# Scattering a group's expert outputs back to tokens in fp32r high and low parts instead of fp32

## The chip, the cores and the metric

One core of a Trainium2 chip runs the whole kernel. The time is device microseconds of one execution; what counts is the median of the runs. A profiled execution gives the span (first to last instruction) and its own time.

## The reference

Two transformer blocks run one after the other over 256 tokens of width 1024. The first block ends in a mixture of experts: four groups of eight experts, a router picks one group for each token and two experts in it, and the weighted outputs are added to the tokens. Cut to what matters here:

```
g_sel = argmax(softmax(t @ w_rg + b_rg))            # one of 4 groups
top_p, top_i = top_k(softmax(e_logits of g_sel), 2) # two of its 8 experts
combine = one_hot(global_idx) * weights             # [tokens, 32]
for e in range(32):
    hid = silu(t @ w_gate[e]) * (t @ w_up[e])       # 1024 -> 256
    out = out + combine[:, e:e+1] * (hid @ w_down[e])   # 256 -> 1024
h = h + gt2 * out
```

After it come a final norm of the first block, then the second block: feed-forward passes (1024 to 2816 and back) over context and latents, attention, a convolution mixer and two more passes.

## The kernel before

**Weights.** All weights come as pages of 128 x 2048 fp32 (1 MB). A page for a three-product matmul is split: ScalarE (ACT) copies it to fp32r as the high part, GpSimd (POOL) subtracts that from the page and gives the low part, and TensorE (PE) forms high x high, high x low and low x high. The queue of SP issues the page loads in one written order, each behind waits on semaphores for the space it needs.

**The experts' stage.** Tokens are sorted by group into five groups of 128 rows (GSLOTS = 5, numbered j), and each group goes through the eight experts of its weights: 40 units (NUNIT), u = 8 j + e. A unit takes three expert pages (gate/up in two parts, and the down page), and in 32 of the 40 units (MOD_UNITS: all of the first 36 but every ninth) a modulation page (`mraw`) as well, which VectorE (DVE) multiplies by a vector and sums over k (`mod_sum`, into `MACC`), TensorE sums over partitions (`mod_product`) and VectorE adds to a table (`mod_take`). From unit 13 on the modulation pages are summed for two vectors, before for one.

TensorE's order in unit u (lines 1160 to 1186) is: first half of gate/up of u, transposing the hidden part of u-1, second half of gate/up of u, down of u-1 (fp32, 8 instructions of 512 columns, line 1146), `mod_product` of the page before, then one item of the groups' work: for group j-1 one quarter of the scatter (`scatter`, e = 1 to 4), or for group j+1 a gather (e = 5, 6) or `aux` (e = 7).

**The groups' work.** `onehot(j)` on VectorE writes the one-hot matrix EM (rows of a group by tokens), `gather` multiplies by it, `aux` transposes it in TensorE and `aux_copy` copies it to ET. After a group's last expert its outputs stand in PSUM banks 0 and 1, [128 rows, 1024]. `out_copy` on ScalarE copies them to OS in SBUF in two halves (line 1576), in unit 8(j+1) behind that unit's silu and two page splits. `scatter(j, r)` on TensorE multiplies quarter r of OS (two blocks of 128 columns as stationary operand) by ET (256 tokens), one fp32 matmul for each block, into bank 5; the profile shows an fp32 matmul as two instructions. `add_tokens(j, r)` on VectorE adds the result to the residual HT (line 2172), and each further quarter waits for the addition of the one before (semaphore s_scd). The fifth group has no unit behind it: its four quarters (`last_scatter`, line 1088) stand in the first feed-forward pass, between the first page's gate matmuls and the second's, and VectorE's `residual` takes them.

VectorE's order in unit u (lines 2184 to 2211) is: the hidden product HID (line 2191), `mod_sum` and `mod_take`, `add_tokens` (e = 1 to 4), `onehot` (e = 4), `gathered_lo` (e = 5, 6), `aux_copy` (e = 7). TensorE's `down(u)` for e = 0 waits until the banks were copied out (s_os), and `mod_product(m)` waits for `MACC` of page m (s_macc) and for the table entry before it (s_modev).

Of the kernel before, what the change touches and what calls it, by code (L numbers as in the profile page):

```python
# [20 lines left out]
P = 128  # L21
D = 1024
KD = D // P
S = 256
# [6 lines left out]
NG, NE8 = 4, 8  # L31
# [55 lines left out]
GSLOTS = S // P + NG - 1  # L87
# [5 lines left out]
def build(nc, pages, mpages, acts, vecs, mbias, small):  # L93
    f32, f32r, bf16, i32 = mybir.dt.float32, mybir.dt.float32r, mybir.dt.bfloat16, mybir.dt.int32
    ALU, ACT, AX = mybir.AluOpType, mybir.ActivationFunctionType, mybir.AxisListType

    ctx = ExitStack()
    with ctx:
        def sb(name, shape, dt=f32):
            return ctx.enter_context(nc.sbuf_tensor(name, shape, dt))  # L100
# [3 lines left out]
        def sem(name):  # L104
            if name not in sems:
                sems[name] = ctx.enter_context(nc.semaphore(name))
            return sems[name]
# [44 lines left out]
        LAMT = sb("LAMT", [P, 8])  # L152
        LAMV = MSK[:].rearrange("p (a b) -> p a b", a=4)
        ST = sb("ST", [P, 32])
        R = sb("R", [P, 11008])

        def reg(off, *dims, parts=P):
            n = int(np.prod(dims))
            v = R[0:parts, off:off + n]
            names = "abcd"[:len(dims)]  # L160
            if len(dims) == 1:
                return v
            return v.rearrange(f"p ({' '.join(names)}) -> p {' '.join(names)}",
                               **{names[i]: dims[i] for i in range(1, len(dims))})
# [19 lines left out]
        YT = reg(4096, TB, D)  # L184
        RW = reg(8192, 8, 80)
        EM = reg(8832, TB, P)
        ET = reg(9088, 2, S)
        OS = reg(9600, D)
        CWS = reg(10624, GSLOTS, NE8)
        IOTA, TRI, PIDX = CTf[:, 0:P], CTf[:, P:2 * P], CTf[:, 2 * P:2 * P + 1]  # L190
        GI = RW[:, 7, 64:64 + GSLOTS].bitcast(i32)
# [59 lines left out]
        def bias_of(h):  # L251
# [20 lines left out]
        s_mhi, s_mlo = sem("expert_page_hi"), sem("expert_page_lo")  # L272
        s_gu, s_gsil, s_ghid, s_gturn, s_ght, s_gdown = (sem("expert_gate_up"), sem("expert_silu"), sem("expert_hid"),
                                                         sem("expert_turned"), sem("expert_hid_copied"), sem("expert_down"))
        s_os, s_sct, s_scd = sem("group_out_copied"), sem("group_scattered"), sem("group_added")
        s_em, s_gat, s_xh, s_xl, s_aux, s_auxd = (sem("group_onehot"), sem("group_gathered"), sem("group_hi"), sem("group_lo"),
                                                  sem("group_aux"), sem("group_aux_copied"))
        s_silu = sem("silu_done")
# [160 lines left out]
        def opened(pe, name, i=0):  # L439

            if prev_free[name, i] is not None:
                pe.wait_ge(*prev_free[name, i])
            return bank(name, i)
# [226 lines left out]
        def _(pe):  # L670
# [388 lines left out]
            def aux(j):  # L1059
# [9 lines left out]
                              skip_group_check=True)  # L1069
                last.then_inc(s_aux, 1)  # L1070

            def scatter(j, r):
                if r == 0:
                    pe.wait_ge(s_os, 2 * (j + 1))
                    pe.wait_ge(s_auxd, 2 * (j + 2))
                else:
                    pe.wait_ge(s_scd, 4 * j + r)
                for b in range(2):
                    last = mm(PS[SPARE][:, b * S:(b + 1) * S], OS[:, (2 * r + b) * P:(2 * r + b + 1) * P], ET[:, j % 2, :],
                              start=True, stop=True, skip_group_check=True)  # L1080
                last.then_inc(s_sct, 1)

            def last_scatter():
                pe.wait_ge(s_os, 2 * GSLOTS)
                for r in range(4):
                    ps = opened(pe, "acc_moe", r)
                    for b in range(2):
                        last = mm(ps[:, b * S:(b + 1) * S], OS[:, (2 * r + b) * P:(2 * r + b + 1) * P],
                                  ET[:, (GSLOTS - 1) % 2, :], start=True, stop=True, skip_group_check=True)
                    last.then_inc(s_tile, 1)  # L1090

            def gate_up(u, ks):
                ps, x = PS[GATE_UP[u % 2]], (XGH[u // NE8 % 2], XGL[u // NE8 % 2])
# [44 lines left out]
            def down(u):  # L1138
                pe.wait_ge(s_ght, u + 1)
                pe.wait_ge(sem(f"expert_down_in_{u % 2}"), 16 * (u // 2 + 1))  # L1140
                if u % NE8 == 0 and u:
                    pe.wait_ge(s_os, 2 * (u // NE8))
                w = down_page(u)
                for j in range(2):
                    for n in range(2):
                        last = mm(PS[OUT[n]][:, :], HTT[:, j, :], w[:, j * D + n * 512:j * D + n * 512 + 512],  # L1146
                                  start=(u % NE8 == 0 and j == 0), stop=(u % NE8 == NE8 - 1 and j == 1), skip_group_check=True)
                last.then_inc(s_gdown, 1)
# [232 lines left out]
        def _(act):  # L1381
# [189 lines left out]
            def out_copy(j):  # L1571
                act.wait_ge(s_gdown, NE8 * (j + 1))
                if j:
                    act.wait_ge(s_sct, 4 * j)
                for n in range(2):
                    f(OS[:, n * 512:(n + 1) * 512], PS[n][:, :], ACT.Copy).then_inc(s_os, 1)

            for a in range(4):
                act.wait_ge(sem("tokens_turned"), a + 1)
# [147 lines left out]
        def _(dve):  # L1727
            v = nc.vector
# [18 lines left out]
            def mod_sum(m, vectors, i=0):  # L1747

                w = mraw[:, m % 2, :].rearrange("p (k n) -> p k n", k=KD)
                dve.wait_ge(mslot[m % 2], i * 16 + 16 * (m // 2 + 1 - MOD_AT["gates"] // 2))  # L1750
                if m:
                    dve.wait_ge(s_macc, i * 2 + m)
                for k in range(KD):
                    if k:

                        dve.wait_ge(s_mx, i * 2 * (KD - 1) + ((KD - 1) * m + k))
                    for slot_v, vi in enumerate(vectors):
                        part, c = PS[MISC][:, slot_v * FU:(slot_v + 1) * FU], CA[:, k, vi:vi + 1]
                        out = MACC[:, m % 2, slot_v, :] if k == KD - 1 else part
                        if k == 0:  # L1760
                            last = v.tensor_scalar(out, w[:, k, :], c, None, ALU.mult)
                        else:
                            last = v.scalar_tensor_tensor(out=out, in0=w[:, k, :], scalar=c, in1=part,  # L1763
                                                          op0=ALU.mult, op1=ALU.add)
                    last.then_inc(s_mx if k < KD - 1 else s_macc, 1)
# [69 lines left out]
            def modcol(c, vi=0):  # L1835
                return lambda k: MODT[:, c + k, vi:vi + 1]
# [318 lines left out]
            def gathered_lo(j, r):  # L2155
                dve.wait_ge(s_xh, 2 * j + r + 1)
                ps = PS[3] if j == 0 and r == 1 else PS[5]
                k = slice(4 * r, 4 * r + 4)
                v.tensor_tensor(XGL[j % 2][:, k, :], ps[:, :].rearrange("p (k n) -> p k n", k=4),
                                XGH[j % 2][:, k, :].bitcast(f32), ALU.subtract).then_inc(s_xl, 1)  # L2160
# [7 lines left out]
            def add_tokens(j, r):  # L2168
# [4 lines left out]
                                                  scalar=MODT[:, ADA + 40 + k, 0:1], in1=HT[:, k, :], op0=ALU.mult, op1=ALU.add)  # L2173
                last.then_inc(s_scd, 1)

            gathered_lo(0, 0)
            gathered_lo(0, 1)
            for n, (u, part) in enumerate(EARLY):
# [5 lines left out]
            for u in range(NUNIT):  # L2184
                j, e = u // NE8, u % NE8
                dve.wait_ge(s_gsil, u + 1)
                if u:
                    dve.wait_ge(s_gturn, u)
                if e == 0:
                    dve.wait_ge(s_auxd, 2 * (j + 1))  # L2190
                v.scalar_tensor_tensor(out=HID, in0=SIL[:, u % 2, :].rearrange("p (j n) -> p j n", j=2), scalar=CWS[:, j, e:e + 1],
                                       in1=PS[2 + u % 2][:, :].rearrange("p (j g n) -> p j g n", j=2, g=2)[:, :, 1, :],
                                       op0=ALU.mult, op1=ALU.mult).then_inc(s_ghid, 1)
                if u == 0:
                    mod_sum(20, (0,))
                if u in MOD_UNITS:
                    k = MOD_UNITS.index(u)
                    vectors = (0,) if k < MOE_ADA else (1, 2)
                    mod_sum(MOD_AT["moe"] + k, vectors)
                    mod_take(MOD_AT["moe"] + k - 1, 0, len(vectors))  # L2200
                if j and 1 <= e <= 4:
                    if e == 1 and j == 1:
                        dve.wait_ge(s_modev, (ADA + 48) // 2)
                    add_tokens(j - 1, e - 1)
                if j + 1 < GSLOTS:
                    if e == 4:
                        onehot(j + 1)
                    elif e in (5, 6):
                        gathered_lo(j + 1, e - 5)
                    elif e == 7:  # L2210
                        aux_copy(j + 1)
                if u == NUNIT - 3:
                    norm_head(2)
                if u == NUNIT - 2:
                    norm_tiles(2, range(0, 5), low=False)
                if u == NUNIT - 1:
                    norm_tiles(2, range(5, KD), low=False)
                    for q in range(KD):
                        norm_low(2, q)
            residual("acc_moe", (HT, modcol(ADA + 40)))  # L2220


# [304 lines left out]
```

## Time and profile before

| | |
|---|---|
| runs | 2069.66, 2064.40, 2061.06 us; median 2064.4 |
| profiled execution | 2073.07 us, span 2071.3 us, granted clock 0.979 |
| TensorE busy | 1976.6 us, 95% of the span |
| GpSimd busy | 1379.1 us, 67% |
| VectorE busy | 981.7 us, 47% |
| ScalarE busy | 827.7 us, 40% |
| DMA | 473.80 MB, mean 229 GB/s |
| experts' stage | from about 250 to 715 us of the span |

Busy times of one engine overlap with those of others. A matmul's duration is longer than the distance to the next one, since they are pipelined; what a matmul costs is the distance of starts. PEld is the load of the stationary operand. A clock of 1.00 is TensorE's full 2.4 GHz.

### The profile page before, as it was taken

To read this page: it belongs to the slowest core of one execution; us is meant where nothing else is said; L and a number is where in the kernel's file an instruction comes from. 1 tells how busy PE (TensorE), PEld (TensorE's weight loads), DVE (VectorE), ACT (ScalarE), POOL (GpSimd) and SP (SyncE) were. 2 spreads that over 40 slices of the span, in tenths; PEclk is the share of its full clock that TensorE was granted. 3 is DMA by queue.
4 is the path that set the end of the run, shared out by engine and by line. 5 is a ranking of instruction groups with operands and counts; after the bars stand their busy time and mean duration, and the time that the engine had idled before them with its cause. 6 is when DMAs were issued, how large, how long until landed. Compare 5 with 4: busy or idle time off the path is not lost.

```text
span 2071.3 us, 34705 instructions
## 1 busy us (share of the span) xinstructions
PE 1976.6 (95%) x13854; PEld 1780.4 (86%) x13854; DVE 981.7 (47%) x2149; ACT 827.7 (40%) x873; POOL 1379.1 (67%) x321
## 2 busy tenths in 40 slices
PE   6999799999999999999999999899999999999998
PEld 4879766677676799999999768689999999999998
DVE  6766453567676354345335243453335334642112
ACT  4443344444434554334434333343344334434332
POOL 5727078778778677787775412277776776766884
PEclk9999899999999999999999999999999999999999
DMA  8636299989998656665664302156665565554542
GB/s 354 227 121 265 100 359 365 372 343 377 360 382 334 257 204 227 241 243 217 250 236 167 123 27 96 45 220 244 242 236 200 237 236 229 221 187 160 184 182 82
DMA packets 67407, 473.80 MB, mean 229 GB/s; under 512 B 8064, under 2 KB 9184, under 8 KB 10208
## 3 DMA queue, kind: packets, MB, share of 16 engines
q1 hardware_dynamic: 65344, 466.82, 59.0%
q10 hardware_dynamic: 1952, 5.44, 0.7%
q8 instruction: 78, 1.28, 0.2%
q14 instruction: 33, 0.27, 0.0%
HBM read 471.18 MB, written 1.05 MB: 228 GB/s over the span
## 4 chain that ended last, share of the span: by engine, by line
PE 49%; issue 23%; POOL 18%; DMA 5%; DVE 2%; ACT 1%; SPq 0%; POOLq 0%; ACTq 0%; DVEq 0%
POOL W L606 15%; PE bank L675 11%; PE bank L677 11%; PE bank L676 11%; PE bank L1146 4%; DMA raw<-in_pages 4%; PE bank L681 2%; PE bank L683 2%; PE bank L682 2%; POOL YC L657 2%; POOL W L657 1%; PE bank L709 1%; PE bank L700 1%; PE bank L1055 1%; DMA mraw<-in_mpages 1%
## 5 line engine op out<-in xcount | busy, mean ns | idle before, releaser
L606 POOL TENSOR_TENSOR W<-raw,W 128x2048 fp32r<-128x2048 f32 x220 | 1013.9, 4613 | 528.9 <-ACT W L1436 528.8
L675 PE MATMUL bank<-YH,W 128*128 128x256 f32 x1936 | 551.2, 285 | 1.4 <-POOL W L606 1.1
L677 PE MATMUL bank<-YH,W 128*128 128x256 f32 x1936 | 547.7, 283 | 0.0
L676 PE MATMUL bank<-YL,W 128*128 128x256 f32 x1936 | 547.6, 283 | 0.0
L1436 ACT ACTIVATE W<-raw 128x2048 fp32r<-128x2048 f32 x220 | 420.2, 1910 | 300.6 <-PE bank L677 274.6
L675 PEld LDWEIGHTS bank<-YH,W 128*128 128x128 f32 x1936 | 371.1, 192 | 4.2 <-POOL W L606 1.5
L676 PEld LDWEIGHTS bank<-YL,W 128*128 128x128 f32 x1936 | 371.3, 192 | 0.4 <-issue 0.2
L677 PEld LDWEIGHTS bank<-YH,W 128*128 128x128 f32 x1936 | 371.2, 192 | 0.0
L1763 DVE SCALAR_TENSOR_TENSOR bank<-mraw,CA,bank 128x256 f32<-128x256 f32 x702 | 331.5, 489 | 20.3
L1860 DVE TENSOR_TENSOR bank<-bank,SIL 128x256 f32<-128x256 f32 x110 | 47.6, 432 | 574.6 <-ACT SIL L1455 574.6
L675 PE MATMUL bank<-HH,W 128*128 128x256 f32 x880 | 249.4, 283 | 0.4 <-DVE HL L1862 0.4
L677 PE MATMUL bank<-HH,W 128*128 128x256 f32 x880 | 245.7, 279 | 0.0
L676 PE MATMUL bank<-HL,W 128*128 128x256 f32 x880 | 245.3, 279 | 0.0
L657 POOL TENSOR_TENSOR W<-raw,W 128x2048 fp32r<-128x2048 f32 x38 | 173.2, 4580 | 84.6 <-ACT W L1558 84.6
L1558 ACT ACTIVATE W<-raw 128x2048 fp32r<-128x2048 f32 x79 | 151.2, 1915 | 147.1 <-DMA raw<-in_pages 147.1
L657 POOL TENSOR_TENSOR YC<-raw,W 128x2048 fp32r<-128x2048 f32 x36 | 163.9, 4576 | 43.9 <-ACT W L1558 43.9
L1455 ACT ACTIVATE SIL<-bank 128x256 f32<-128x256 f32 x110 | 42.2, 384 | 361.6 <-PE bank L677 359.3
L681 PE MATMUL bank<-W,YH 128*128 128x512 f32 (+1 forms) x392 | 154.4, 394 | 14.7 <-POOL YC L657 7.3
L675 PEld LDWEIGHTS bank<-HH,W 128*128 128x128 f32 x880 | 165.7, 188 | 0.6 <-issue 0.4
L676 PEld LDWEIGHTS bank<-HL,W 128*128 128x128 f32 x880 | 165.6, 188 | 0.0
L677 PEld LDWEIGHTS bank<-HH,W 128*128 128x128 f32 x880 | 165.4, 188 | 0.0
L675 PE MATMUL bank<-YC,W 128*128 128x256 f32 (+1 forms) x536 | 153.6, 287 | 1.0 <-DVE R L1950 1.0
(348 smaller groups left out, 3130.9 us busy)
## 6 DMA issues: line engine op xcount, KB each, us to landing
raw<-in_pages SPq DMA_DIRECT2D x299, 1024.0 KB, 4.9
mraw<-in_mpages SPq DMA_DIRECT2D x98, 1024.0 KB, 7.0
R<-in_pages SPq DMA_DIRECT2D x24, 1024.0 KB, 6.3
XR<-in_pages SPq DMA_DIRECT2D x17, 1024.0 KB, 6.3
R<-in_mpages SPq DMA_DIRECT2D x4, 1024.0 KB, 16.4
HT<-in_acts ACTq DMA_DIRECT2D x1, 1024.0 KB, 14.2
CT<-in_mpages SPq DMA_DIRECT2D x1, 1024.0 KB, 19.4
raw<-in_mpages SPq DMA_DIRECT2D x1, 1024.0 KB, 25.2
```

The costliest lines, as they stand in the source:

```text
L606: nc.gpsimd.tensor_tensor(WL[:, p % SLOTS, :], raw[:, p % SLOTS, :], WH[:, p % SLOTS, :].bitcast(f32), ALU.subtract).then_inc(s_lo, 1)
L657: p_.tensor_tensor(PAIRL[u % 2][:, part].rearrange("p k n -> p (k n)"), expert_raw(u, part), PAIRH[u % 2][:, part, :].bitcast(f32), ALU.su ...
L675: mm(out, w[0], x[0], start=start, stop=False, skip_group_check=True)
L676: mm(out, w[0], x[1], start=False, stop=False, skip_group_check=True)
L677: return mm(out, w[1], x[0], start=False, stop=stop, skip_group_check=True)
L681: mm(out, x[0], w[0], start=start, stop=False, skip_group_check=True)
L1146: last = mm(PS[OUT[n]][:, :], HTT[:, j, :], w[:, j * D + n * 512:j * D + n * 512 + 512], start=(u % NE8 == 0 and j == 0), stop=(u % NE8 == ...
L1436: f(WH[:, p % SLOTS, :], raw[:, p % SLOTS, :], ACT.Copy).then_inc(s_hi, 1)
L1455: f(SIL[:, j, :], PS[GU[j]][:, 0:S], ACT.Silu).then_inc(s_silu, 1)
L1558: f(PAIRH[u % 2][:, part, :], expert_raw(u, part), ACT.Copy).then_inc(s_mhi, 1)
L1763: last = v.scalar_tensor_tensor(out=out, in0=w[:, k, :], scalar=c, in1=part, op0=ALU.mult, op1=ALU.add)
L1860: step(v.tensor_tensor(hid, hid, sil, ALU.mult))
```

## The change

The scatter's two operands become fp32r. ScalarE's copy of the group's outputs writes fp32r (OSH), VectorE gets a new step `out_low` that subtracts it from the PSUM banks and writes the low part (OSL, fp32r), and each scatter block is two fp32r matmuls, high and low, against one ET, which is fp32r now too (its copy on VectorE writes that type). RR is a second name for the memory of R; OSL lies in a part of it that the stage does not use. What waited on s_os for the copies (scatter's first quarter, `down` of a group's first unit, the last scatter) waits on s_osl for the subtractions. `out_low(j-1)` stands in VectorE's order behind HID of unit 8j and ahead of that unit's `mod_sum`; for the last group it stands ahead of `residual`.

```diff
-        ET = reg(9088, 2, S)
-        OS = reg(9600, D)
+        ET = RR[:, 9088:9600].rearrange("p (a t) -> p a t", a=2)
+        OSH, OSL = RR[:, 9600:9600 + D], RR[:, 2048:2048 + D]
...
+            def to_tokens(ps, j, r):
+                for b in range(2):
+                    k = 2 * r + b
+                    mm(ps[:, b * S:(b + 1) * S], OSH[:, k * P:(k + 1) * P], ET[:, j % 2, :], start=True, stop=False,
+                       skip_group_check=True)
+                    last = mm(ps[:, b * S:(b + 1) * S], OSL[:, k * P:(k + 1) * P], ET[:, j % 2, :], start=False, stop=True,
+                              skip_group_check=True)
+                return last
+
             def scatter(j, r):
                 if r == 0:
-                    pe.wait_ge(s_os, 2 * (j + 1))
+                    pe.wait_ge(s_osl, 2 * (j + 1))
                     pe.wait_ge(s_auxd, 2 * (j + 2))
                 else:
                     pe.wait_ge(s_scd, 4 * j + r)
-                for b in range(2):
-                    last = mm(PS[SPARE][:, b * S:(b + 1) * S], OS[:, (2 * r + b) * P:(2 * r + b + 1) * P], ET[:, j % 2, :],
-                              start=True, stop=True, skip_group_check=True)
-                last.then_inc(s_sct, 1)
+                to_tokens(PS[SPARE], j, r).then_inc(s_sct, 1)

             def last_scatter():
-                pe.wait_ge(s_os, 2 * GSLOTS)
                 for r in range(4):
...
+                    if r % 2 == 0:
+                        pe.wait_ge(s_osl, 2 * (GSLOTS - 1) + r // 2 + 1)
+                    to_tokens(opened(pe, "acc_moe", r), GSLOTS - 1, r).then_inc(s_tile, 1)
...
                 if u % NE8 == 0 and u:
-                    pe.wait_ge(s_os, 2 * (u // NE8))
+                    pe.wait_ge(s_osl, 2 * (u // NE8))
...
-                    f(OS[:, n * 512:(n + 1) * 512], PS[n][:, :], ACT.Copy).then_inc(s_os, 1)
+                    f(OSH[:, n * 512:(n + 1) * 512], PS[n][:, :], ACT.Copy).then_inc(s_os, 1)
...
+            def out_low(j):
+                if j:
+                    dve.wait_ge(s_sct, 4 * j)
+                for n in range(2):
+                    half = slice(n * 512, (n + 1) * 512)
+                    dve.wait_ge(s_os, 2 * j + n + 1)
+                    v.tensor_tensor(OSL[:, half], PS[n][:, :], OSH[:, half].bitcast(f32), ALU.subtract).then_inc(s_osl, 1)
...
                 if u == 0:
                     mod_sum(20, (0,))
+                if j and e == 0:
+                    out_low(j - 1)
                 if u in MOD_UNITS:
...
+            out_low(GSLOTS - 1)
             residual("acc_moe", (HT, modcol(ADA + 40)))
```

## Rows read from the trace of the kernel before

**Rows 1.** Page, parts 1 and 4: busy times; the chain by engine.

```profile
PE 1976.6 (95%) x13854; PEld 1780.4 (86%) x13854; DVE 981.7 (47%) x2149; ACT 827.7 (40%) x873; POOL 1379.1 (67%) x321
...
PE 49%; issue 23%; POOL 18%; DMA 5%; DVE 2%; ACT 1%; SPq 0%; POOLq 0%; ACTq 0%; DVEq 0%
```

**Rows 2.** Windows: engines' busy us (instructions), PE clock, DMA share, GB/s; experts' stage.

```profile
350.00:430.00 80.00, 75.98 (x314) 55.16 (x313) 45.91 (x89) 33.45 (x31) 67.35 (x15) 0.96 0.90 352
430.00:520.00 90.00, 89.32 (x387) 63.71 (x386) 63.91 (x145) 38.87 (x37) 73.06 (x17) 1.00 0.92 369
...
600.00:710.00 110.00, 104.01 (x429) 72.96 (x430) 57.82 (x133) 53.03 (x58) 79.49 (x20) 0.98 0.81 317
...
730.00:900.00 170.00, 169.63 (x1403) 168.66 (x1401) 74.56 (x163) 76.31 (x74) 127.70 (x29) 1.00 0.62 229
```

**Rows 3.** Timeline of PE: start, us, what, count; the last scatter and after.

```profile
714.64 3.61 PE L1088 MATMUL bank<-R 128*128 128x256 f32 x16
717.90 0.47 PE L675 MATMUL bank<-YC,W 128*128 128x256 f32 x1
718.21 0.28 PE L676 MATMUL bank<-YC,W 128*128 128x256 f32 x1
...
720.48 0.28 PE L677 MATMUL bank<-YC,W 128*128 128x256 f32 x1
```

**Rows 4.** Timeline of PE: units 17 and 25, then later starts behind waits [idle].

```profile
450.76 3.60 PE L1146 MATMUL bank<-R,WRT 128*128 128x512 f32 x8
454.19 0.95 PE L700 MATMUL bank<-ONES,MACC 128*128 128x1 f32 x8
...
466.85 0.50 PE L681 MATMUL bank<-W,YH 128*128 128x512 f32 x1 [0.68 <-POOL YC L657]
...
542.50 0.95 PE L700 MATMUL bank<-ONES,MACC 128*128 128x1 f32 x8
...
567.04 0.50 PE L681 MATMUL bank<-W,YH 128*128 128x512 f32 x1 [1.39 <-POOL W L657]
...
569.19 0.39 PE L681 MATMUL bank<-W,YH 128*128 128x512 f32 x1
...
624.86 0.80 PE L681 MATMUL bank<-W,YH 128*128 128x512 f32 x1 [1.91 <-POOL YC L657]
...
628.53 0.40 PE L681 MATMUL bank<-W,YH 128*128 128x512 f32 x1
...
635.65 0.50 PE L700 MATMUL bank<-ONES,MACC 128*128 128x1 f32 x4
...
666.74 3.70 PE L1146 MATMUL bank<-R,WRT 128*128 128x512 f32 x8 [1.51 <-ACT WRT L1569]
```

**Rows 5.** Timeline of ACT: the output copies of four groups.

```profile
357.07 1.06 ACT L1576 ACTIVATE R<-bank 128x512 f32<-128x512 f32 x2
...
448.08 1.07 ACT L1576 ACTIVATE R<-bank 128x512 f32<-128x512 f32 x2
...
536.26 1.06 ACT L1576 ACTIVATE R<-bank 128x512 f32<-128x512 f32 x2
...
628.07 1.06 ACT L1576 ACTIVATE R<-bank 128x512 f32<-128x512 f32 x2
```

**Rows 6.** Timeline of DVE: sum in unit 16, one-hots of units 12 and 28.

```profile
399.94 4.16 DVE L2123 TENSOR_SCALAR R<-R 128x2 f32<-128x2 f32 x1
...
441.71 0.86 DVE L1761 TENSOR_SCALAR bank<-mraw,CA 128x256 f32<-128x256 f32 x2
...
448.11 0.87 DVE L1763 SCALAR_TENSOR_TENSOR MACC<-mraw,CA,bank 128x256 f32<-128x256 f32 x2
...
583.32 4.70 DVE L2125 TENSOR_SCALAR R<-CT,R 128x128 f32<-128x128 f32 x2
```

**Rows 7.** Groups of DVE by form: the like of the new subtraction.

```profile
L2159 DVE TENSOR_TENSOR YL<-bank,YH 128x512 fp32r<-128x512 f32 x10 | 6.9, 685 | 8.3 <-ACT YH L1563 8.3
```

**Rows 8.** Timeline of POOL: the two page subtractions beside unit 28's one-hot.

```profile
578.62 9.12 POOL L657 TENSOR_TENSOR W<-raw,W 128x2048 fp32r<-128x2048 f32 x2 [2.56 <-ACT W L1558]
```

More of the change, by code:

```diff
@@ L154, in build @@
         ST = sb("ST", [P, 32])
+        with nc.sbuf_tensor("RR", [P, 11008], f32r) as RR:
+            pass
         R = sb("R", [P, 11008])
@@ L274, in build @@
                                                          sem("expert_turned"), sem("expert_hid_copied"), sem("expert_down"))
-        s_os, s_sct, s_scd = sem("group_out_copied"), sem("group_scattered"), sem("group_added")
+        s_os, s_osl, s_sct, s_scd = (sem("group_out_high"), sem("group_out_low"), sem("group_scattered"),
+                                     sem("group_added"))
         s_em, s_gat, s_xh, s_xl, s_aux, s_auxd = (sem("group_onehot"), sem("group_gathered"), sem("group_hi"), sem("group_lo"),
@@ L1077, in scatter @@
                     pe.wait_ge(s_scd, 4 * j + r)
-                for b in range(2):
-                    last = mm(PS[SPARE][:, b * S:(b + 1) * S], OS[:, (2 * r + b) * P:(2 * r + b + 1) * P], ET[:, j % 2, :],
-                              start=True, stop=True, skip_group_check=True)
-                last.then_inc(s_sct, 1)
+                to_tokens(PS[SPARE], j, r).then_inc(s_sct, 1)
             def last_scatter():
-                pe.wait_ge(s_os, 2 * GSLOTS)
                 for r in range(4):
[L1086 to L1090, printed above, removed]
+                    if r % 2 == 0:
+                        pe.wait_ge(s_osl, 2 * (GSLOTS - 1) + r // 2 + 1)
+                    to_tokens(opened(pe, "acc_moe", r), GSLOTS - 1, r).then_inc(s_tile, 1)
             def gate_up(u, ks):
```

## The prediction

> **What bounds the kernel now.** I read the page first, for the bound as a whole: TensorE is busy 95% of the span, POOL 67%, and the chain that ended last is half TensorE [rows 1]. Then the windows, because the change lies in the experts' stage only, from about 260 to 720 us. There TensorE is busy 76.0 of 80 us, 89.3 of 90 and 104.0 of 110, while the DMA engines are busy 81 to 92% and move 317 to 369 GB/s [rows 2]. So two limits stand close together in this stage: TensorE sets the end of most units, and now and then a page lands late and TensorE waits for POOL's low part. The reader is to see those waits in TensorE's timeline: 0.68 us at 466.85, 1.39 at 567.04, 1.91 at 624.86, 1.51 at 666.74 [rows 4]. Behind the stage TensorE is the bound outright, 169.6 of 170 us [rows 2].
>
> **TensorE's part of the change.** The last scatter has 16 instructions (8 fp32 matmuls of two each). From its first start at 714.64 to that of the fp32r matmul behind it at 717.90 are 3.26 us, 0.204 each; with the odd step to 718.21 in it, less one fp32r distance, 3.45 us, 0.216 each. I take 0.21 us [rows 3]. An fp32r matmul of the same shape goes at the distance of starts of the pass behind it: 19 steps from 718.21 to 720.48, 0.1195 us [rows 3]. The new form has as many instructions as the old, since each block is a high and a low matmul: 4 in place of 4 in a quarter, 16 in place of 16 in the last scatter. Each loses 0.21 - 0.12 = 0.09 us. A quarter saves 0.36 us, 16 quarters save 5.8 us, the last scatter saves 1.44 us: 7.2 us in all. The bounds are 0 (if fp32r with these operands went at fp32's 0.21 us) and 7.2; I take 7.2, since the neighbouring row is of the same shape and type. The Trainium skill, page TensorE: Matmul & The Clock Gate, section "Wait — 56ns, not 53.3ns?", gives a warm distance of the columns over 2.4 GHz and some 2.5 ns, 109 ns for 256 columns. The rows say 0.1195, and the measurement decides; by the page the whole saving would be an estimated 0.8 us larger.
>
> ScalarE's copy only changes its output type, and so does VectorE's copy to ET: both cost nothing, hidden as before.
>
> **VectorE's part.** `out_low` adds two subtractions of 128x512 from PSUM to fp32r for each group, ten in all. The like of it takes 685 ns, with a mean over ten instances [rows 7]: 1.37 us a group, 6.9 us in all. VectorE is 47% busy [rows 1] and 63.9 of 90 us in its fullest window [rows 2], so the work itself is hidden. What counts is where it waits. It waits for ScalarE's copies, which run far behind the unit's silu, because two page splits stand ahead of them: they start at 357.07, 448.08, 536.26 and 628.07 and take 1.06 us [rows 5]. Behind the waiting `out_low` stands the unit's `mod_sum`, and for it waits `mod_product` on TensorE one unit later.
>
> Unit 16: `mod_sum` ran from 441.71 to 448.98, 7.27 us [rows 6]. Now the first copy (half of 1.07 us) is there at 448.6, the subtractions end at 448.6 + 1.37 = 450.0, the sum runs to 457.3. TensorE's `down` of that group at 450.76 finds its banks free 0.8 us before it needs them. Its `mod_product` stood at 454.19 [rows 4] and now waits until 457.3: 3.1 us. Unit 24: copies from 536.26, subtractions to 538.2, sum to 545.5; `mod_product` stood at 542.50 [rows 4, 5]: 3.0 us. Unit 32: 628.07, 630.0, 637.3, against 635.65: 1.6 us. Unit 8: subtractions to 359.0, a sum for one vector behind them, and unit 9 has no page and so no product: no wait. Sum of the new waits: 7.7 us.
>
> After a wait the clock may fall. Behind the 1.91 us of idle, nine starts from 624.86 to 628.53 took 3.67 us, at half clock for most of them; behind the 1.39 us of idle, nine starts from 567.04 to 569.19 took 2.15 us [rows 4]. So a fall costs 1.5 us. I charge it for the two waits of 3 us and not for the one of 1.6, which lies between an idle of 1.51 without a fall and one of 1.91 with it.
>
> What else is late behind VectorE's delay is covered: HID of unit 17 comes behind the sum, near 458, and the transposing that needs it stands in TensorE's order behind `mod_product` (now 457.3), a scatter and half a gate/up. `add_tokens` of the first quarter stands behind one more sum of 7.3 us, near 466; the second quarter stood just ahead of 466.85 [rows 4] and the stall moves it too. The SP queue holds page loads behind `s_macc` of two pages before; these sums are done long before their turn. For the last group `out_low` ends at 710.5 on an idle VectorE, and the scatter cannot start before the first page's gate matmuls end at 714.64 [rows 3]: nothing.
>
> **Sum, by group.** Quarters of group 0 (units 9 to 12): -1.44, but the page behind unit 12 and the one-hot behind it (4.16 us of waiting in its first instruction [rows 6]) set the next start, so I keep -0.7. Group 1: +3.1 wait, +1.5 clock, -0.68 because the wait at 466.85 is swallowed, -1.44 scatters: +2.5. Group 2: +3.0 + 1.5 - 1.39 (the wait at 567.04) - 1.44: +1.7. Group 3: TensorE arrives later by then, so half of the 1.91 + 1.5 us around 624.86 goes: -1.7; its own wait of 1.6, less three quarters' gain, vanishes in the 1.51 us at 666.74; the fourth quarter gives -0.36. Last scatter: -1.44, kept in full, since TensorE bounds what follows [rows 2]. Together -0.7 + 2.5 + 1.7 - 1.7 - 0.36 - 1.44 = 0.0 us. The profiled execution would stay at 2073 us, 8.7 us above the runs' median (0.4%); on the median that is 2064.4 + 0.0, so about 2064 us: no change.
>
> **Rivals.**
> A. The waits do not form (VectorE's sums keep their lead, or the pages of these units land so late that TensorE is not there to wait), and the gain is kept: 2064.4 - 7.2 = 2057.2 us. For it: VectorE idles much. Against: `mod_sum` of unit 16 ended only 5.2 us before its use [rows 4, 6], and it moves by 8.3.
> B. The waits are paid in full: three waits of 7.7 us, three falls of the clock of 4.5 us, nothing covered, against 7.2 gained: +5.0, 2069.4 us. For it: the kernel issues the next pages behind TensorE's `down`, so a late TensorE makes the pages late too. It decides from the point where the waits at 567.04 and 624.86 come back as long as before.
> C. The one-hot on VectorE falls behind one more subtraction of POOL. The row of unit 28: two small instructions take 4.70 us and end at 588.0 just behind POOL's pair, which ended at 587.74, 4.56 us for each [rows 6, 8]; the gather on TensorE stands right behind them. VectorE's order moves against POOL's by some us, and where it gets to the one-hot just after POOL has started another page, TensorE waits up to 4.56 + 1.5 us. Twice, on top of the forecast: +12.1, 2076.5 us: the case on the other side, slower. Against: by units 20 and 28 VectorE has caught up, and POOL's times follow the same pages. The Trainium skill, page SBUF — State Buffer, section "Who interferes with whom", has the rule for this: an operation such as tensor_scalar in a two-port mode and a GpSimd instruction exclude one another for a whole instruction. The trace agrees, by the 4.70 and 4.16 us.
> D. The change doesn't do what it says: fp32r products with these operands take fp32's time, and 7.2 us go missing: 2071.6 us. Against: 0.1195 us in every fp32r pass of this shape.
>
> **Chances.** Forecast (2061 to 2068) 0.60, A 0.13, B 0.14, C 0.08, D 0.05. A measurement of this kernel can tell about 0.5%, 10.3 us, from no change: below 2054.1 or above 2074.7. A lies inside that unless chance runs add to it; the three runs of before spread from -3.3 to +5.3 us about their median. Faster 0.08, same 0.80, slower 0.12 (C and the upper end of B and D). The range of 8 in 10 is 2056 to 2073: it takes in A and B with their spread, and leaves out C.
>
> **What would show it.** Right: L1079's and L1088's successors as fp32r at 0.12 us each, the last scatter at 1.9 us in place of 3.4; ten new VectorE subtractions of 0.69 us; an idle of TensorE ahead of `mod_product` (L700 in before's numbering) in units 17 and 25 near 3 us, released by VectorE's MACC, with half clock behind it; the waits in units 19 and 28 gone. Wrong: no such idle and an experts' stage shorter by 6 us (A); the old waits unchanged beside the new (B); a gather waiting for the one-hot (C).

## The result: slower by 0.67%

The changed kernel took 2080.54 us (median of 6 runs, 2079.34 to 2085.12), the kernel before 2066.3 us (6 runs, 2061.06 to 2071.89). The ratio is 1.0067, 95% interval 1.005 to 1.0084: some 14 us slower, where 2064 us and no change were forecast, with a range up to 2073. The profiled execution took 2080.16 us, span 2078.3 us, granted clock 0.977.

### The profile page after: what moved, and what is told of

Its sections match the earlier page's. It is cut to its first block, busy times and chain, and to the rows that moved or that the text cites. A ratio compares the mean times of both kernels' runs of the same rounds, so it can differ in the third digit from the quotient of the medians.

```text
span 2078.3 us, 34720 instructions
## 1 busy us (share of the span) xinstructions
PE 1975.6 (95%) x13854; PEld 1779.9 (86%) x13854; DVE 993.1 (48%) x2159; ACT 826.6 (40%) x873; POOL 1379.3 (66%) x321
## 4 chain that ended last, share of the span: by engine, by line
PE 46%; issue 24%; POOL 18%; DMA 6%; DVE 4%; ACT 1%; SPq 0%; POOLq 0%; ACTq 0%; DVEq 0%
POOL W L609 15%; PE bank L678 11%; PE bank L680 11%; PE bank L679 11%; DMA raw<-in_pages 4%; PE bank L1152 3%; PE bank L684 2%; PE bank L685 2%; PE bank L686 2%; DVE bank L1769 2%; POOL YC L660 1%; DMA mraw<-in_mpages 1%; PE bank L712 1%; PE bank L703 1%; POOL W L660 1%
## 5 line engine op out<-in xcount | busy, mean ns | idle before, releaser
L684 PE MATMUL bank<-W,YH 128*128 128x512 f32 (+1 forms) x392 | 152.9, 390 | 11.8 <-DVE W L2194 4.3
```

The lines of the kernel that those rows point to most:

```text
L684: mm(out, x[0], w[0], start=start, stop=False, skip_group_check=True)
```

## The profile after

The page's first and fourth part, as in [rows 1]. TensorE has the same number of instructions and is busy for 1 us less; VectorE has ten instructions more and 11 us more. The chain has less TensorE in it (46% for 49%) and more VectorE (4% for 2%).

```profile
PE 1975.6 (95%) x13854; PEld 1779.9 (86%) x13854; DVE 993.1 (48%) x2159; ACT 826.6 (40%) x873; POOL 1379.3 (66%) x321
...
PE 46%; issue 24%; POOL 18%; DMA 6%; DVE 4%; ACT 1%; SPq 0%; POOLq 0%; ACTq 0%; DVEq 0%
```

TensorE's work in the last scatter, from its timeline, against [rows 3]: 16 instructions from 725.86 on, 15 steps in 1.79 us, 0.119 us each. This term of the sum is as forecast.

```profile
725.86 0.28 PE L1078 MATMUL bank<-RR 128*128 128x256 f32 x1
...
727.65 0.28 PE L1080 MATMUL bank<-RR 128*128 128x256 f32 x1
```

The new subtractions, from the groups of VectorE (busy, mean ns | idle before, by what). They cost what [rows 7] said, 686 ns. The 39.3 us are VectorE's waits for ScalarE's copies.

```profile
L2188 DVE TENSOR_TENSOR RR<-bank,RR 128x512 fp32r<-128x512 f32 x10 | 6.4, 686 | 39.3 <-ACT RR L1582 39.3
```

Where TensorE waited between 250 and 720 us: the view of waits, after (us in total, times, longest). L703 is the modulation product, L1152 the down matmuls, L684 gate/up, L1058 the gather.

```profile
PE bank L703 <- DVE MODT L1778: 10.1, 3, 3.6
PE bank L684 <- DVE W L2194: 4.3, 1, 4.3
PE bank L684 <- POOL YC L660: 3.7, 4, 1.9
PE bank L1152 <- DVE RR L2188: 3.6, 3, 1.4
PE bank L684 <- POOL W L660: 3.6, 3, 1.7
PE bank L1058 <- DVE R L2131: 2.8, 2, 1.6
PE bank L1152 <- ACT WRT L1575: 1.1, 1, 1.1
```

And before:

```profile
PE bank L681 <- POOL YC L657: 7.3, 4, 2.3
PE bank L681 <- DVE W L2180: 4.3, 1, 4.3
PE bank L1146 <- ACT WRT L1569: 3.3, 3, 1.5
PE bank L681 <- POOL W L657: 3.1, 2, 1.7
PE bank L1055 <- DVE R L2125: 1.7, 1, 1.7
```

Two lines are new, 10.1 us at the product and 3.6 us at the down matmuls. Those for POOL and ScalarE went from 13.7 to 8.4 us, so it looks as if 5.3 us of the new waits replace old ones. That is a comparison of one profile with one; two more profiles of the changed kernel, from the experiments below, have 9.7 + 0.8 us (`e1_after`) and 10.4 + 2.2 us (`e4_after`) of new waits beside 7.3 and 9.8 us of old ones. The wait at the product is the steady part.

How one such wait comes about: units 16 and 17 after, first ScalarE, then VectorE, then TensorE (start, us, what; in brackets the idle before).

```profile
439.26 0.38 ACT L1601 ACTIVATE SIL<-bank 128x256 f32<-128x256 f32 x1 [1.62 <-PE bank L686]
445.03 1.92 ACT L1564 ACTIVATE W<-raw 128x2048 fp32r<-128x2048 f32 x1 [5.38 <-DMA raw<-in_pages]
447.62 1.92 ACT L1564 ACTIVATE W<-raw 128x2048 fp32r<-128x2048 f32 x1 [0.67 <-DMA raw<-in_pages]
449.44 1.06 ACT L1582 ACTIVATE RR<-bank 128x512 fp32r<-128x512 f32 x2
```

```profile
450.12 1.29 DVE L2188 TENSOR_TENSOR RR<-bank,RR 128x512 fp32r<-128x512 f32 x2 [9.96 <-ACT RR L1582]
451.33 0.86 DVE L1767 TENSOR_SCALAR bank<-mraw,CA 128x256 f32<-128x256 f32 x2
...
457.73 0.87 DVE L1769 SCALAR_TENSOR_TENSOR MACC<-mraw,CA,bank 128x256 f32<-128x256 f32 x2
458.51 0.15 DVE L1778 TENSOR_TENSOR MODT<-bank,MB 128x4 f32<-128x4 f32 x1
```

```profile
451.56 3.67 PE L1152 MATMUL bank<-R,WRT 128*128 128x512 f32 x8 [1.45 <-DVE RR L2188]
458.82 1.17 PE L703 MATMUL bank<-ONES,MACC 128*128 128x1 f32 x8 [3.59 <-DVE MODT L1778]
459.85 0.56 PE L1078 MATMUL bank<-RR 128*128 128x256 f32 x1
460.20 0.41 PE L1080 MATMUL bank<-RR 128*128 128x256 f32 x1
...
460.85 0.63 PE L684 MATMUL bank<-W,YH 128*128 128x512 f32 x1
...
462.98 0.39 PE L686 MATMUL bank<-W,YH 128*128 128x512 f32 x1
```

ScalarE's copies stand behind two page splits, and those behind the landing of their pages: 10.2 us after unit 16's silu. VectorE idles 9.96 us for them with the modulation sum queued behind. TensorE first waits for the subtractions at the down matmuls (1.45 us), then for the sum at the product (3.59 us). Unit 33 shows the same pair, 1.29 and 3.59 us. The second number is the same because, once the down matmuls are held by the subtractions, both engines start from there: the sum and its table entry take 7.3 us, the down matmuls 3.7 us, and the difference is TensorE's wait. Behind it the clock is at half: the scatter's steps are 0.21 us, no faster than fp32 was. So are the first gate/up matmuls, 0.42 us a step until 462.98 and 0.23 behind.

From one unit's silu to the next is the length of a unit. I add the stage from unit 0's silu to unit 39's (before 263.68 to 698.96, after 265.65 to 710.18).

| kernel (one profile each) | 17 to 18 | 25 to 26 | 33 to 34 | stage |
|---|---|---|---|---|
| before | 10.95 | 10.95 | 10.95 | 435.3 |
| before, product later (`e3_before_late`) | 10.90 | 10.89 | 10.89 | 430.6 |
| changed | 17.13 | 15.25 | 18.69 | 444.5 |
| changed, again (`e1_after`) | 16.68 | 17.01 | 16.98 | 445.7 |
| changed, again (`e4_after`) | 15.53 | 18.68 | 17.38 | 445.1 |

## The experiments

Theory W: it is VectorE's order. The subtraction waits for the copies, the sum waits behind it, TensorE waits for both. Rival P: the time goes elsewhere; a faster scatter moves TensorE against the pages, and the pages set the end. Every comparison is with the kernel before on the same chip.

**The changed kernel again**, twice, unedited (`e1_after`, `e4_after`).

> The changed kernel as it is, beside the next three. Theory W (order of VectorE): the low subtraction waits some 10 us for ScalarE's copies with the modulation sum behind it, TensorE then waits at the down matmuls and at the modulation product of units 17, 25 and 33, some 4 to 8 us a time. Both theories: about 2080 us, ratio 1.007 to the kernel before.

2084.02 us, ratio 1.0058 (1.0035 to 1.0081); stage 445.7 us.

**Subtractions behind the sum** (`e1_behind`).

```diff
-                if j and e == 0:
-                    out_low(j - 1)
                 if u in MOD_UNITS:
...
                     mod_take(MOD_AT["moe"] + k - 1, 0, len(vectors))
+                if j and e == 0:
+                    out_low(j - 1)
```

> out_low moved behind mod_sum and mod_take in VectorE's order, nothing else. Theory W: the waits at the modulation product vanish; the copies end some 10 us after the silu and the sum some 8 to 9 us after it, so the subtractions are done hardly later than now and a wait of 1 to 3 us at the down matmuls may stay; 2062 us, between 2057 and 2067, ratio 0.996 to 1.001. Rival P (the time goes elsewhere: the faster scatter shifts TensorE against the pages' landing and the pages set the end): no change from 2080 us.

2065.66 us, ratio 0.9993 (0.9981 to 1.0006). The whole loss is gone with an order of two steps, and nothing of the scatter was touched: P falls. No line for the product is left in the waits; the down matmuls wait 0.2 us for the subtractions. Units 17, 25 and 33 take 10.54, 10.58 and 10.94 us, the stage 430.4.

**Copies ahead of the page splits** (`e1_copyfirst`).

```diff
+                j, e = u // NE8, u % NE8
+                if j and e == 0:
+                    out_copy(j - 1)
                 if u + 2 < NUNIT:
                     expert_split(u + 2, 0)
                     expert_split(u + 2, 1)
-                j, e = u // NE8, u % NE8
-                if j and e == 0:
-                    out_copy(j - 1)
```

> ScalarE's out_copy moved ahead of the unit's two page splits, VectorE's order as in the changed kernel. Theory W: the copies no longer wait for pages; they start when the down matmuls of the group before end, 3.5 us after the silu, the sum ends about 13 us after the silu and the product is wanted at about 14: all waits gone, 2060 us, between 2056 and 2066. If the two splits start later by it (the pages land 2.3 us or more after the silu), up to 2 us a group come back. Rival P: 2080 us.

2064.19 us, ratio 0.9982 (0.9966 to 0.9997). VectorE's order is the changed kernel's, so it was not that the subtraction stood ahead of the sum, but that it waited there for copies held by pages. In unit 16 VectorE's idle is now 3.24 us, and the product does not wait:

```profile
442.78 1.29 DVE L2188 TENSOR_TENSOR RR<-bank,RR 128x512 fp32r<-128x512 f32 x2 [3.24 <-ACT RR L1582]
...
450.38 0.87 DVE L1769 SCALAR_TENSOR_TENSOR MACC<-mraw,CA,bank 128x256 f32<-128x256 f32 x2
```

```profile
452.71 0.95 PE L703 MATMUL bank<-ONES,MACC 128*128 128x1 f32 x8
```

**VectorE's part alone, in the kernel before** (`e1_lowonly`): fp32 scatter; the low values are computed and waited for, and nothing reads them.

```diff
+                    v.tensor_tensor(OSL[:, half], PS[n][:, :], OS[:, half], ALU.subtract).then_inc(s_osl, 1)
...
-                    pe.wait_ge(s_os, 2 * (j + 1))
+                    pe.wait_ge(s_osl, 2 * (j + 1))
...
+                if j and e == 0:
+                    out_low(j - 1)
```

> The kernel before with VectorE's low subtraction added and waited for as in the changed kernel, but the scatter stays fp32 and reads the high part's place (OS in fp32) alone; the low values are written and read by nothing. Theory W: it has all of the loss and none of the gain of 7 us: 2085 to 2092 us, ratio 1.010 to 1.014. Rival P: no loss without the faster scatter, 2066 us.

2080.07 us, ratio 1.0053 (1.0032 to 1.0073); waits at the product 8.9 us in three, stage 446.9. The loss is there without the fp32r scatter. I had expected 2085 to 2092 us, the changed kernel's time and the missing gain of 7 us on top, and that did not come: the ratio is level with `e1_after`'s 1.0058, each with an interval of some 4 us to either side. While the waits stand, the scatter's gain does not show in this comparison; no run says why.

**The gain side alone** (`e2_highonly`).

```diff
-                    last = mm(ps[:, b * S:(b + 1) * S], OSL[:, k * P:(k + 1) * P], ET[:, j % 2, :], start=False, stop=True,
+                    last = mm(ps[:, b * S:(b + 1) * S], OSH[:, k * P:(k + 1) * P], ET[:, j % 2, :], start=False, stop=True,
...
-                    pe.wait_ge(s_osl, 2 * (j + 1))
+                    pe.wait_ge(s_os, 2 * (j + 1))
...
-                if j and e == 0:
-                    out_low(j - 1)
```

> The changed kernel without VectorE's low subtraction: it leaves the low part out and takes the high part in its place, so the scatter has the same number of fp32r matmuls, and its waits are those of the kernel before (on ScalarE's copies). This is the gain side alone. Theory W with the forecast's size: 80 instructions at 0.12 in place of 0.21 us, -7.2 us at most, 2060 us, ratio 0.996 to 0.998. Rival P (in this stage the pages set the end, so a shorter scatter is given back): -1.5 us, what the last scatter gives, ratio 0.999 to 1.000.

2063.2 us, ratio 0.9968 (0.9953 to 0.9983), which is 6.6 us, 3.5 to 9.7. The forecast's 7.2 us lie inside, and the 1.5 us of rival P outside. The low part is left out here, so this kernel is only good for its time.

**Product half a gate/up later** (`e2_late`), and its controls without the change (`e3_before_late`) and with the fp32 scatter and unread low values (`e3_lowonly_late`).

```diff
+            def product(u):
+                k = MOD_UNITS.index(u)
+                mod_product(MOD_AT["moe"] + k - 1, 0, 1 if k < MOE_ADA else 2)
...
                     gate_up(u, range(0, KD // 2))
+                    if u > 10 and u % NE8 == 2 and u - 1 in MOD_UNITS:
+                        product(u - 1)
                     turn_hid(u - 1)
...
-                if u in MOD_UNITS:
-                    k = MOD_UNITS.index(u)
-                    mod_product(MOD_AT["moe"] + k - 1, 0, 1 if k < MOE_ADA else 2)
                 j, e = u // NE8, u % NE8
+                if u in MOD_UNITS and not (u > 9 and e == 1):
+                    product(u)
```

> The changed kernel with TensorE's modulation product of units 17, 25 and 33 put half a gate/up later (behind scatter and the first half of the next unit's gate/up, 3.2 us). VectorE's order is left as it is. If the wait at the product is the larger part of the loss, most of it goes: 2070 us (2066 to 2074). If the wait at the down matmuls and the fall of the clock behind it carry the loss, it stays at 2078 to 2084.

> The kernel before with TensorE's product of units 17, 25 and 33 half a gate/up later: the control for e2_late. The sum is done 5 us before the product is wanted there, so nothing should change: ratio 0.999 to 1.001. If it gives 0.998 as e2_late did, that gain is the order's and not the scatter's.

> The kernel before with VectorE's low subtraction (fp32 scatter, the low values read by nothing) and the product half a gate/up later. With e1_lowonly it says how much of the subtraction's loss is the product's wait, with e2_late what the fp32r scatter gives once that wait is gone. Theory W: the loss of 12 us shrinks to 0 to 3 us, 2068 to 2071 us, ratio 1.000 to 1.0015, and the fp32r scatter is worth the 4 to 6 us between this and e2_late. If the scatter's gain is given back to the pages in any case, it comes out level with e2_late, 0.998.

`e2_late`: 2065.19 us, ratio 0.9981 (0.9968 to 0.9993), better than the 2070 expected. VectorE is as late as ever, a wait at the down matmuls stays (1.1 us in two, 0.83 of it in unit 17), and of the wait at the product 0.39 us is left:

```profile
450.39 3.67 PE L1152 MATMUL bank<-R,WRT 128*128 128x512 f32 x8 [0.83 <-DVE RR L2193]
457.65 1.02 PE L703 MATMUL bank<-ONES,MACC 128*128 128x1 f32 x8 [0.39 <-DVE MODT L1783]
```

So the wait at the product, with what follows it, is the loss. `e3_before_late`: 2068.15 us, 1.0008 (0.9994 to 1.0021): the order by itself gives nothing. `e3_lowonly_late`: 2067.19 us, 1.0000 (0.9985 to 1.0015). Against `e2_late` the fp32r scatter is worth 0.0019, some 4 us; the two intervals overlap a little.

**Both mends** (`e2_both`, again as `e4_both`), **the copies' order without the change** (`e2_before_copyfirst`), **all three mends** (`e3_allthree`, again as `e4_allthree`). Their diffs are those above.

> Both mends together: copies ahead of the page splits and subtractions behind the modulation sum. Theory W: no wait is left that either removes, so no better than the better of the two alone by more than 1 us; 2063 us, ratio 0.997 to 0.999.

> The kernel before with ScalarE's out_copy ahead of the unit's page splits, nothing of the change. If that order is worth something by itself, the gain of the mended changed kernel is not the scatter's: 2064 us or less. I expect no change, ratio 0.999 to 1.001, since the copies ended before the down matmuls needed the banks.

> The changed kernel with copies ahead of the splits, subtractions behind the sum, and the product half a gate/up later. No wait is left for the third mend to remove: as e2_both, 2062 us, ratio 0.997 to 0.998.

> Copies ahead of the splits and subtractions behind the sum, again: ratio 0.997 to 0.998 as before, 2062 to 2063 us.

> The same with the product half a gate/up later, again: 0.998 to 1.000. Its trace of the run before shows units 17, 25 and 33 at 12.4 us against 11.6, 11.6 and 10.7 with both mends alone; if that is real and not one execution's phase, it stays 2 to 4 us above e4_both.

Both mends: 2062.45 us, 0.9975 (0.9959 to 0.9991), and 2064.44 us, 0.9986 (0.9969 to 1.0003); stage 426.7 and 427.0 us. The copies' order without the change: 2065.94 us, 0.9988 (0.9975 to 1.0001), stage 430.6. So a gain of the change with both mends over the old scatter is not shown clear of noise: the control without the change has 0.9988 on the chip where both mends had 0.9975, and the intervals overlap. All three: 2067.32 us, 0.9998 (0.9983 to 1.0012), and 2066.67 us, 0.9992 (0.9974 to 1.001). I had expected the third mend to do nothing; it seems to cost 1 to 5 us (units 17, 25 and 33 took 12.4 to 13.2 us in its two profiles, with both mends alone 10.7 to 11.6), but the intervals touch. The profiles show where: in these units TensorE waits 0.8 to 1.6 us at gate/up for POOL's part of a page (with both mends 0 to 0.7), and in some of them 0.8 to 1.2 us at the down matmuls for the subtractions. Why POOL is later there is open.

```profile
455.27 0.50 PE L684 MATMUL bank<-W,YH 128*128 128x512 f32 x1 [1.61 <-POOL W L660]
```

**Subtractions done twice** (`e3_double`).

```diff
+                    v.tensor_tensor(RR[:, 3072 + n * 512:3584 + n * 512], PS[n][:, :], OSH[:, half].bitcast(f32), ALU.subtract)
```

> The changed kernel with each low subtraction done twice (the first into memory that nothing reads), so the modulation sum behind it starts 1.3 to 1.4 us later in units 8, 16, 24 and 32. Theory W: TensorE's waits for it in units 17, 25 and 33 and for the subtractions at the down matmuls grow by that much, and nothing covers it: +4 to +5.5 us over the changed kernel, 2084 to 2090 us, ratio 1.008 to 1.011. Rival P: no change, 2080 to 2083.

2081.88 us, ratio 1.0082 (1.0063 to 1.01): by the ratio 3 us above the changed kernel's 1.0067, with overlapping intervals, and by the medians not above `e1_after`. Its stage took 445.1 us, as the changed kernel's. The dose is too small for its measurement. Inconclusive.

**TensorE kept at work in the wait** (`e4_fill`), beside `e4_after`.

```diff
+                if e == 1 and j > 1:
+                    pe.wait_ge(s_auxd, 2 * (j + 1))
+                    for _ in range(16):
+                        mm(PS[SPARE][:, 0:P], IDENT[:], ONES[:], start=True, stop=True, skip_group_check=True)
```

> The changed kernel again, as the partner of e4_fill: 2080 to 2084 us, ratio 1.006 to 1.008.

> The changed kernel with 16 small fp32 matmuls (identity by ones, 128 columns, into the idle bank 5, read by nothing; some 3.5 us) on TensorE ahead of the modulation product of units 17, 25 and 33, where it waits about 3 to 3.6 us anyway. If the fall of the clock behind the wait carries 1.5 to 1.9 us a time, it ends 3 to 6 us below the changed kernel, ratio 1.004 to 1.005. If the clock's fall costs nothing on the way to the end, it ends level or up to 1 us above.

`e4_after`: 2080.93 us, 1.0072 (1.0045 to 1.01). `e4_fill`: 2073.95 us, 1.0038 (1.0023 to 1.0054). Useless work in the same wait makes the kernel 7.0 us faster by the medians. The two intervals overlap a little, but both stand on the same runs of before; of the twelve filled runs eight are below the fastest of the six unfilled. The windows around the three groups (us, then busy us and instructions of TensorE, weight load, VectorE, ScalarE and GpSimd, granted clock, DMA share, GB/s), first `e4_after`:

```profile
436.00:476.00 40.00, 36.51 (x147) 25.96 (x146) 21.76 (x53) 16.90 (x17) 33.99 (x8) 0.96 0.82 325
528.00:568.00 40.00, 35.20 (x137) 24.76 (x136) 25.58 (x63) 16.64 (x16) 30.27 (x7) 0.91 0.85 317
620.00:660.00 40.00, 36.11 (x141) 25.31 (x140) 25.51 (x62) 15.60 (x16) 28.05 (x7) 0.91 0.95 380
```

then `e4_fill`:

```profile
436.00:476.00 40.00, 40.00 (x183) 29.10 (x182) 21.43 (x54) 15.76 (x17) 34.69 (x8) 1.00 0.86 344
528.00:568.00 40.00, 40.00 (x190) 29.87 (x189) 27.79 (x69) 15.57 (x18) 31.93 (x8) 1.00 0.95 366
620.00:660.00 40.00, 37.00 (x174) 26.89 (x173) 28.53 (x70) 17.15 (x17) 33.52 (x8) 1.00 0.89 343
```

The clock column is the point: 0.96, 0.91, 0.91 against 1.00 three times. Units 17, 25 and 33 took 14.12, 14.12 and 15.00 us, mean 14.4, where the three profiles of the changed kernel have 15.3 to 18.7, mean 17.0. That is 2.6 us a time, 7.9 us in all, and the time moved by 7.0. (The profile of `e4_fill` is of the longest of its twelve runs, 2078.25 us; its stage took 439.8 us, against 445.1 in `e4_after`.)

A unit's length also holds the wait at the down matmuls, so I take the clock's part alone as well: from the product's start to the next transposing (L1141), where nothing is waited for. In unit 17, first of the kernel of the result, then of `e4_fill` (L1183 is the useless work):

```profile
458.82 1.17 PE L703 MATMUL bank<-ONES,MACC 128*128 128x1 f32 x8 [3.59 <-DVE MODT L1778]
...
464.58 0.38 PE L1141 MATMUL bank<-IDENT,MSK 128*128 128x128 f32 x2
```

```profile
453.30 3.73 PE L1183 MATMUL bank<-ONES,IDENT 128*128 128x128 f32 x32
456.87 0.95 PE L703 MATMUL bank<-ONES,MACC 128*128 128x1 f32 x8
...
460.98 0.38 PE L1141 MATMUL bank<-IDENT,MSK 128*128 128x128 f32 x2
```

5.76 against 4.11 us here. The nine such stretches in the three profiles of the changed kernel take 5.76 to 7.37 us, mean 6.67, the three of `e4_fill` 4.11 to 4.18: 2.5 us a time, between 1.6 and 3.2. The length of the idle does not tell which: behind the same 3.59 us in one profile unit 17 took 5.76 and unit 33 7.37 us.

## Why the prediction was wrong

1. **The price of the instructions: right.** 0.12 us for fp32r in the last scatter, 0.686 us for a subtraction, ScalarE's copy at 585 ns, unchanged. The gain of 7.2 us: 6.6 measured without VectorE's part.
2. **The place and the mechanism: right.** `out_low` waiting for the copies with `mod_sum` behind it, `mod_product` late in units 17, 25 and 33 and not in unit 9: all in the trace. What failed is the cost: the prediction set it off against gain and cover to zero.
3. **The size of the waits: the first failed step.** The forecast was 7.7 us at the product and none at the down matmuls; measured were 10.1 + 3.6 = 13.7 us, and 10.5 and 12.6 in the two other profiles. The product's waits in units 17 and 25 were sized about right, 2.9 to 3.6 us for 3.1 and 3.0. Two terms were not. "TensorE's `down` of that group finds its banks free 0.8 us before it needs them" was wrong: there were three waits, 3.6 us (one in unit 9), and one and two, 0.8 and 2.2 us, in the other profiles. And in unit 33 the product waited 3.59 us in all three profiles, not 1.6: unit 32's old numbers held a TensorE that POOL had kept until 624.86 [rows 4], and in the changed kernel POOL kept it there for only 0.2 to 0.3 us. Behind both is one fault: the prediction took the copies' times, 448.08, 536.26 and 628.07, from the old trace as fixed, and TensorE's beside them. Both move. The copies hang on page landings: their lag behind unit 16's silu was 7.2 us before, and 10.2, 7.1 and 7.7 in the three profiles of the changed kernel.
4. **The clock: the second failed step.** 1.5 us for two waits, 3.0 us in all, were taken from the nine starts behind one idle of 1.9 us [rows 4]. Behind the longer idle the product and the scatter ran at half clock as well, and it happened in all three units: 7.9 us by the units of `e4_fill`, 7.6 by the stretches. This is the larger miss.
5. **What swallows it: booked somewhat too high.** 4.3 us were booked: 0.68, 1.39, 1.7, and of the 1.51 us at 666.74 the 0.5 that were left of unit 33's wait. In the pair of profiles of the result the old waits shrank by 5.3. With points 3 and 4 the stage's sum would have been 13.7 + 7.9 - 5.3 - 5.8 (the 16 quarters) = +10.5 us, against +9.2 measured there (444.5 less 435.3). That this comes out so near is in part luck, by the next point.
6. **The base: one long execution.** The profile of before took 2073.07 us, 6.8 above its median of six. Its stage was 435.3 us, while the two controls without the change (`e2_before_copyfirst`, `e3_before_late`), which measure like it, have 430.6. Part of the waits that were to swallow the loss were of that execution and not of the kernel: neither control has one in the place of the 0.68 us at 466.85 or of the 1.51 us at 666.74, one of the two has 0.92 us for the 1.39 at 567.04, and only the 1.91 us at 624.86 is in both (1.92 and 1.94). From 430.6 the changed kernel's 444.5 to 445.7 is +14 to +15 us, which is the measured loss. The account against the two controls, with means of the three profiles of the changed kernel: new waits +12.3, clock +7.9, old waits for POOL and ScalarE 8.5 where the controls have 11.3 (-2.8), waits of the gather for the one-hot 3.9 where they have 1.6 (+2.3), quarters -5.8: +13.9 us, measured +14.5. So some 3 us were swallowed, not 5.3. The account is an estimate: waits of one kind differ by 2 to 3 us from one profile of the same kernel to the next, and the -5.8 is the forecast's own figure, which `e1_lowonly` does not confirm while the waits stand. That before's profile is just that much longer by chance is an inference from these controls; it was profiled once.
7. **The rivals.** B had the right direction: paid in full. It gave +5.0 since it used the same too small terms. A, the gain kept in full, would be a ratio of 0.9965 (2057.2 to 2064.4 us); with one or both of the two mends it is 0.9975 to 0.9993, and only the interval of `e2_both` takes A in. C, a one-hot behind POOL, is in the trace in the small (2.8 us of gather waits, 4.8 and 4.0 in the other two profiles, 1.7 before), but the mended kernels have 0.6 to 4.5 us of it too, so it is not what the loss hangs on. D did not happen.

## What to carry to other kernels

A wait put into an engine's queue costs what stands behind it, not what it does itself: ask what the waiting instruction's releaser waits for in its turn, here ScalarE's page splits and through them the DMA. Do not take absolute times for two engines from one trace and subtract: what is anchored to a page landing moves against what is anchored to TensorE, so price the wait over the whole spread of the lag. Where TensorE is the bound, an idle of 3 us is to be booked at nearly double (here 3.4 us of idle and 2.5 behind it, on the mean), and a step that nobody needs at once belongs behind the wait: moving two steps turned 1.0067 into 0.9975 to 0.9986. And take a second profile of the base before old waits are booked as cover: here one profile stood 4.7 us above its controls in the stage alone.

## What the runs showed of the hardware that I had not expected

Idles of TensorE of 2.9 to 3.6 us cost another 1.6 to 3.2 us each, 2.5 on the mean, by the half clock behind them, at the level of 1.2 GHz, and idles of the same 3.59 us cost different amounts. 32 useless small instructions in the same wait (3.6 us, matmul of identity by ones) kept the granted clock at 1.00 and took 7.0 us off the whole time. At half clock fp32r of 256 columns goes at 0.21 us a step, the pace of an fp32 instruction at full clock.
